# One MLP stage for two blocks: 1024 tokens with one Strassen level, u through DRAM

## The reference

```python
h = rms_norm(x, norm_mix[i])
m = rms_norm(mem, norm_mem[i])
y_mix, xq = gla_branch(h, gla_w_in[j], gla_w_gate2[j], gla_b_gate[j], gla_out_gain[j])
y_mem = memory_cross_attention(xq, m, w_kv[i])
x = x + jnp.concatenate([y_mix, y_mem.astype(y_mix.dtype)], axis=-1) @ w_out[i]
x = x + sq_relu_mlp(rms_norm(x, norm_mlp[i]), w_up[i], w_down[i])
return rms_norm(x, final_norm)

def sq_relu_mlp(h, w_up, w_down):
    u = jax.nn.relu(h @ w_up)
    return (u * u) @ w_down
```

## Time and profile before

| | |
|---|---|
| median of 3 runs | 2464.06 us (2461.39 to 2465.43) |
| span of the profiled execution, first to last instruction | 2459.9 us |
| the profiled execution's own time | its span and what lies around it; the median of the runs is 4.2 us above the span |
| TensorE busy | 2441.6 us, 99% |
| DVE busy | 1830.7 us, 74% |
| ACT busy | 1291.8 us, 53% |
| POOL busy | 312.5 us, 13% |
| DMA | 505 MB, 205 GB/s on average |

### The profile page before, as it was taken

The page is one execution under the profiler, slowest core; times in us unless marked ns, Lnnn a source line. Parts: engine busy times, 40 slices in busy tenths (PEclk is TensorE's granted clock), DMA queues, the critical chain, the costliest instruction groups (busy, mean ns, idle before and its releaser), DMA issues.

```text
span 2459.9 us, 34497 instructions
## 1 busy us (share of the span) xinstructions
PE 2441.6 (99%) x12912; PEld 2105.9 (86%) x12912; DVE 1830.7 (74%) x2671; ACT 1291.8 (53%) x2035; POOL 312.5 (13%) x327
## 2 busy tenths in 40 slices
PE   9999999999999999999999999999999999999998
PEld 8888888888788888889988888898898888889987
DVE  6677468778856788777775768877785677887777
ACT  5545354544543456566644345665665435556655
POOL 0033200000303320000020431000020142000000
PEclk9999999999999999999999999999999999999999
DMA  8964548677695444466564626355665553545554
GB/s 317 350 213 172 188 172 313 251 274 258 244 373 211 171 163 133 163 214 209 188 219 175 242 101 202 111 184 203 213 212 203 189 199 122 184 149 177 188 182 179
DMA packets 237843, 505.00 MB, mean 205 GB/s; under 512 B 12432, under 2 KB 125456, under 8 KB 219504
## 3 DMA queue, kind: packets, MB, share of 16 engines
q1 hardware_dynamic: 237248, 502.73, 58.4%
q10 hardware_dynamic: 432, 0.07, 0.0%
HBM read 423.07 MB, written 79.69 MB: 204 GB/s over the span
## 4 chain that ended last, share of the span: by engine, by line
PE 95%; DVE 2%; DMA 2%; issue 1%; ACT 0%; POOL 0%; SPq 0%; DVEq 0%; POOLq 0%; ACTq 0%
PE banks L3026 28%; PE banks L3028 28%; PE banks L3027 28%; PE banks L3216 3%; PE banks L3188 1%; PE banks L3262 1%; PE banks L3256 1%; PE banks L3165 1%; PE banks L3240 1%; DMA sr<-in_w_out 1%; PE banks L3178 0%; PE banks L3482 0%; PE banks L3274 0%; DMA xres<-in_x 0%; PE banks L3099 0%
## 5 line engine op out<-in xcount | busy, mean ns | idle before, releaser
L3026 PE MATMUL banks<-h_hi,w_hi 128*128 128x512 f32 (+1 forms) x1728 | 605.6, 350 | 2.4 <-DMA w_lo<-w_in_lo 0.8
L3028 PE MATMUL banks<-h_hi,w_lo 128*128 128x512 f32 (+1 forms) x1728 | 598.1, 346 | 0.0
L3027 PE MATMUL banks<-h_lo,w_hi 128*128 128x512 f32 (+1 forms) x1728 | 597.9, 346 | 0.0
L2833 DVE TENSOR_TENSOR w_lo<-raw,w_hi 128x1024 fp32r<-128x1024 f32 (+1 forms) x312 | 364.8, 1186 | 56.7 <-ACT w_hi L1861 56.4
L1861 ACT ACTIVATE w_hi<-raw 128x1024 fp32r<-128x1024 f32 (+1 forms) x312 | 300.9, 1003 | 166.7 <-PE banks L3026 59.4
L3026 PEld LDWEIGHTS banks<-h_hi,w_hi 128*128 128x128 f32 x1728 | 327.3, 189 | 44.1 <-issue 3.1
L3028 PEld LDWEIGHTS banks<-h_hi,w_lo 128*128 128x128 f32 x1728 | 327.2, 189 | 40.6
L3027 PEld LDWEIGHTS banks<-h_lo,w_hi 128*128 128x128 f32 x1728 | 327.5, 190 | 39.3
L3026 PE MATMUL banks<-w_hi,u_hi 128*128 128x512 f32 x896 | 350.8, 392 | 1.3 <-ACT w_hi L1401 1.0
L3028 PE MATMUL banks<-w_hi,u_lo 128*128 128x512 f32 x896 | 348.8, 389 | 0.0
L3027 PE MATMUL banks<-w_lo,u_hi 128*128 128x512 f32 x896 | 348.7, 389 | 0.0
(11 more groups left out here) (311 smaller groups left out, 4392.9 us busy)
## 6 DMA issues: line engine op xcount, KB each, us to landing
raw<-w_mix SPq DMA_DIRECT2D x52, 1024.0 KB, 4.8
raw<-in_w_down SPq DMA_DIRECT2D x48, 1024.0 KB, 5.7
raw<-w_up_mix SPq DMA_DIRECT2D x72, 512.0 KB, 4.8
w_hi<-w_in_hi SPq DMA_DIRECT2D x29, 1024.0 KB, 4.9
w_lo<-w_in_lo SPq DMA_DIRECT2D x29, 1024.0 KB, 7.9
raw<-in_w_up SPq DMA_DIRECT2D x28, 1024.0 KB, 5.6
raw<-in_gla_w_in SPq DMA_DIRECT2D x21, 1024.0 KB, 7.5
raw<-in_w_up SPq DMA_DIRECT2D x36, 512.0 KB, 4.1
```

Of the source, the lines that this page charges most:

```text
L2833: nc.vector.tensor_tensor(w_lo[:, i % 2, at], raw[:, i % 2, at], w_hi[:, i % 2, at].bitcast(F32), ALU.subtract).then_inc(lo_split.sem, 1)
L3026: after_chunk(pe.matmul(to, left[0], right[0], start=start, stop=False, skip_group_check=goes_on))
L3027: pe.matmul(to, left[0], right[1], start=False, stop=False, skip_group_check=goes_on)
L3028: return pe.matmul(to, left[1], right[0], start=False, stop=stop, skip_group_check=goes_on)
```

## The change

- The mixers and output projections of two blocks run first, then one MLP for both, `mlp(m)` for m = 0, 1, with 1024 tokens. The two blocks are the two halves of the token side, so each of the seven products of an up chunk is 128 hidden columns by 512 tokens (`up_product`). There are 112 up steps (`UP_STEPS`); chunks 0 to 2 are interleaved, chunks 3 to 15 each go M1, M2, M5, M6, M7, M3, M4. `up_bank` gives the bank: M1, M6, M7 and M4 of a chunk share one, M5 and M3 another, M2 has one of its own.
- ACT and DVE split the weights of one product at a time into a ring of eight slots (`up_high`, `up_low`), five to six steps ahead. DVE makes T1 to T4 from the raw weights every time (`up_sum`); `w_up_mix` is gone. DVE also makes S1 to S4 of h at the start of the stage (`s_sums`, `s_low`).
- u and its sums, seven operands, are stored to DRAM (`store_u`, `store_u_sums`). The down projection then runs over 28 steps (`DOWN_STEPS`, seven products by four quarters of the hidden columns); each step loads 1 MB of weights and 1 MB of u and splits both.
- The sums of `w_down` are made in MLP 0's up stage in 32 halves (`half_mix_load`, `half_mix_sums`, `half_mix_store`); before, they were made in block 0.
- All four blocks have the output projection by seven products. The even block's x rows and h columns wait in DRAM for the MLP (`x_kept`, `h_kept`). After blocks 0 and 2 no MLP follows; POOL scales the next block's columns there (`scale_columns`).

The core of the diff:

```diff
-for _g in range(GROUPS):
-    _first = 0 if _g == 0 else DEPTH * _g + 1
-    MLP += [("up", c) for c in range(_first, min(DEPTH * (_g + 1) + 1, UPS))]
-    MLP += [("down", _g, j) for j in range(len(PRODUCTS))]
-LAST_UP = MLP.index(("up", UPS - 1))
...
-LATE_MLP = []
-for _g in range(GROUPS):
-    for _c in range(DEPTH * _g, DEPTH * (_g + 1)):
-        LATE_MLP += [("up", _c)] if _c < PLAIN_UPS else [("up a", _c), ("up b", _c)]
-    LATE_MLP += [("down", _g, j) for j in range(len(PRODUCTS))]
-LATE_LAST_UP = LATE_MLP.index(("up b", UPS - 1))
...
+MLPS = BLOCKS // 2
+FIRST_UPS = 3
+UP_ORDER = ("M1", "M2", "M5", "M6", "M7", "M3", "M4")
+UP_STEPS = [(c, name) for c in range(FIRST_UPS) for name in ("M1", "M2")]
+UP_STEPS += [(c, name) for name in ("M5", "M6") for c in (2, 1, 0)]
+UP_STEPS += [(c, name) for c in (2, 1, 0) for name in ("M7", "M3", "M4")]
+UP_STEPS += [(c, name) for c in range(FIRST_UPS, UPS) for name in UP_ORDER]
+UP_AT = {step: at for at, step in enumerate(UP_STEPS)}
+UP_DONE = [c for c, name in UP_STEPS if name == "M4"]
+PART = CHUNK // KG
+RING = 2 * CHUNK // PART
+UP_LEAD = 5
+UP_SUMS = [(c, e) for c, name in UP_STEPS if name in ("M1", "M5") for e in ((T1, T3) if name == "M1" else (T2, T4))]
+UP_ENDS = {15: 2, 20: 1, 25: 0, 30: 3, 36: 4, **{UP_AT[c, "M4"] + 1: c for c in range(5, UPS)}}
+S_SUMS_AT = {0: (S1,), 1: (S3, S2), 3: (S4,)}
...
+DOWN_STEPS = [(name, quarter) for name, _, _, _ in PRODUCTS for quarter in range(QUARTERS)]
+DOWN_MIX = 2 * UPS
+DOWN_MIX_AT = {18 + 5 * j // 2: j for j in range(DOWN_MIX)}
...
+def up_bank(c, name):
+    if name == "M2":
+        return 6 + c % 2
+    turn = c if c < FIRST_UPS else (5 - c) % 3
+    return turn + (3 if name in ("M5", "M3") else 0)
...
+            def half_mix_store(j):
+                slot, c, half = j % 2, j // 2, slice(j % 2 * 256, (j % 2 + 1) * 256)
+                sp.wait_ge(half_mix_made, j + 1)
+                sp.dma_start(w_mix[:, c // DEPTH, :, c % DEPTH, half], half_mix[:, slot]).then_inc(half_mix_stored[slot], 16)
...
+            def store_u(m, c):
+                sp.wait_ge(*square_ready.at(m, UP_DONE.index(c)))
+                sp.dma_start(u_kept[:, 0:3, c, :], u[:, 0:3, :]).then_inc(u_stored.sem, 16)
+            def store_u_sums(m, c):
+                sp.wait_ge(*u_sums_ready.at(m, UP_DONE.index(c)))
+                sp.dma_start(u_kept[:, 3:OPERANDS, c, :], u[:, 3:OPERANDS, :]).then_inc(u_sums_stored.sem, 16)
...
+                sp.dma_start(u_raw[slot][:], u_kept[:, operand, DEPTH * quarter:DEPTH * (quarter + 1), :])\
+                    .then_inc(u_loaded[slot].sem, 16)
...
+                    if at - 1 in UP_ENDS:
+                        store_u(m, UP_ENDS[at - 1])
+                    if at - 3 in UP_ENDS:
+                        store_u_sums(m, UP_ENDS[at - 3])
+                    if m == 0 and at + 3 in DOWN_MIX_AT:
+                        half_mix_load(DOWN_MIX_AT[at + 3])
+                    if m == 0 and at - 1 in DOWN_MIX_AT:
+                        half_mix_store(DOWN_MIX_AT[at - 1])
...
+                    act.wait_ge(*up_sum_ready.at(m, UP_SUMS.index((c, operand))))
+                nc.scalar.activation(ring_hi[:, s % RING], up_source(c, operand), ACT.Copy).then_inc(up_hi.sem, 1)
...
+                def make_u(c):
+                    before = UP_DONE.index(c) - 1
+                    if before >= 0:
+                        act.wait_ge(*u_stored.at(m, before))
+                        act.wait_ge(*u_sums_ready.at(m, before))
+                    act.wait_ge(*mlp_full(m, ("up", c, "M4")))
+                    nc.scalar.activation(u[:, A21, :], bank(("up", c, "M4")), ACT.Relu)\
+                        .then_inc(bank_read[bank_of(("up", c, "M4"))], 1)
+                    for name in ("M2", "M7", "M3"):
+                        act.wait_ge(*mlp_read(m, ("up", c, name)))
+                    for e in range(3):
+                        last = nc.scalar.activation(u[:, e, :], up_home(c, e), ACT.Relu)
+                    last.then_inc(relu_ready.sem, 1)
+                    act.wait_ge(*mlp_read(m, ("up", c, "M4")))
+                    nc.scalar.activation(u[:, A21, :], u[:, A21, :], ACT.Square)
+                    act.wait_ge(*relu_ready.at(m, before + 1))
+                    nc.scalar.activation(u[:, 0:3, :], u[:, 0:3, :], ACT.Square).then_inc(square_ready.sem, 1)
...
+                for at, (c, name) in enumerate(UP_STEPS):
+                    if UP_LEAD < at + UP_LEAD + 1 < len(UP_STEPS):
+                        up_high(m, at + UP_LEAD + 1)
+                    if at in S_HIGHS_AT:
+                        s_high(S_HIGHS_AT[at])
+                    if name in ("M1", "M5", "M6"):
+                        keep_part(c, name)
+                    if at in UP_ENDS:
+                        make_u(UP_ENDS[at])
+                    if at == len(UP_STEPS) - 3:
+                        split_down(0)
...
+                                        ring_hi[:, s % RING].bitcast(F32), ALU.subtract).then_inc(up_lo.sem, 1)
...
+                for at, (c, name) in enumerate(UP_STEPS):
+                    for e in S_SUMS_AT.get(at, ()):
+                        s_sums(e)
+                    if at + UP_LEAD < len(UP_STEPS):
+                        up_low(m, at + UP_LEAD)
+                    if at in S_LOWS_AT:
+                        s_low(S_LOWS_AT[at])
+                    if name in ("M2", "M7", "M3"):
+                        add_part(c, name)
+                    if at - 2 in UP_ENDS:
+                        u_sums(UP_ENDS[at - 2])
+                    if m == 0 and at in DOWN_MIX_AT:
+                        half_mix_sums(DOWN_MIX_AT[at])
+                split_down(0)
+                u_sums(UPS - 1)
...
+                        pe.wait_ge(*even_low.at(m, KG - 1 if operand == A11 else KD - 1))
+                    pe.wait_ge(*mlp_empty(m, ("up", c, name)))
+                    high, low = up_operand[operand]
+                    to = bank(("up", c, name))
...
+                for s in range(len(UP_STEPS)):
+                    up_product(s)
+                    if s == 1:
+                        for g in range(KD // 2):
```

2683 lines of the change are left out of this document (1225 added, 1458 removed).

## The result

The changed kernel takes **2505.18 us** (median of 4 runs, 2500.87 to 2506.22), the kernel before, on the same chip, 2462.72 (4 runs, 2459.51 to 2465.43). The ratio is 1.0167 with a 95% interval of 1.0153 to 1.0182: 42 us slower, where 2445 was forecast and 2468 was the top of the range. The profiled executions differ by as much: spans of 2504.4 and 2459.9 us, +44.5.

What follows compares the result with a forecast made beforehand. TensorE, busy 2441.6 of 2459.9 us, was taken as the bound. Savings of 60.8, 8.2 and 1.7 against additions of 24.4, 6.2, 12.4, 6 and 2.8 gave -18.9, with 4.2 around the span 2445 us; range 2412 to 2468.

Steps and rivals of the forecast that it cites:

- What the change takes off: TensorE: up-projection matmuls 60.8 us, block 0's output projection 8.2, two old MLP-stage waits 1.7 saved.
- M6 to M7: Up stages: M7 waits for ACT's copy of M6's bank, 26 times 0.94 us, 24.4 us added (22 to 41).
- u of chunk 3: Chunk 4 of each MLP: making u in ACT's queue delays M7 by 3.1 us, 6.2 added (0 to 8).
- start of the up stage: M5 of chunk 2 waits 6.2 us for DVE's S1 low half in each MLP, 12.4 us added (9 to 18).
- Stage starts: Six places where a DVE, ACT, TensorE chain is rebuilt, 1 us each: 6 us added (3 to 13).
- half sums and DMA: MLP 0's up stage: DMA traffic of u, w_up and w_down's half sums costs 2.8 us (0 to 5.6).
- the clock in MLP 1: TensorE's granted clock: the sum held no loss for it; a fall was only Rival (c).
- rival (b): MLP 0 up: half sums become the bound, 2489 us with a chain of 16.5 us; chance 0.10.
- 3.6 us of slack by the medians: MLP 0's half sums: load 4.4, sum 1.7, store 2.6, with issues about 10 us, in a buffer's turn of 13.6.
- Rival (c): TensorE's clock falls after the two long waits, 4.7 us each, giving 2454 us; chance 0.07.
- Rival (d): Down stages: late u makes the first four steps wait some 5 us each, 2465 to 2485 us; chance 0.07.

Runs made afterwards that it cites:

- the final version: The kernel of experiment 10, timed again: 2432.49 us (4 runs), ratio 0.9875 to the kernel before.
- experiment 1: Changed kernel without the half sums of w_down, their loads and stores; down stages read plain quarters: span 2461.1 us, MLP 0 up 324.1.
- 4: Changed kernel with M7 and M4 in the bank of M5 and M3, computation changed: MLP 1 up 306.2 us instead of 324.2, MLP 0 up 358.2.
- 5: Changed kernel with M2 placed between M6 and M7, banks and computation kept: span 2479.6 us, MLP 1 up 306.0, MLP 0 up 356.3.
- experiment 6: Changed kernel with u of chunk 3 made two steps later and block 0's mixer squares one step earlier: span 2490.2 us, MLP 1 up 319.3.
- experiment 7: Changed kernel with POOL scaling only 64 of 512 columns: output projections of blocks 0 and 2 take 46.4 and 46.1 us instead of 52.3 and 52.7.
- experiment 2: Changed kernel with DVE's half-sum additions on data already in SBUF, no loads or stores: span 2463.8 us, MLP 0 up 324.3.
- experiment 10: Kernel of experiment 9 with the half sums' loads issued by POOL instead of SyncE: span 2430.1 us, MLP 0 up 316.6, MLP 1 up 306.0.
- experiment 9: Changed kernel with the order of 5, the earlier squares, and half sums from step 14 every 2.8 steps: span 2452.5 us, MLP 0 up 336.0.
- experiment 13: Kernel of experiment 10 with DVE instead of POOL scaling the next block's columns in blocks 0 and 2: span 2427.2 us, 2429.0 us in one run.

## Why the prediction was wrong

What the change takes off came as priced. Before's 3408 matmuls of 256 columns, priced at 409.0 us, take 410.3 from start to start, and after's of 512 columns are 227 ns apart wherever nothing waits. So the rows were the right price. The gap of N/2.4 + 2.5 ns that the prediction sets against them is given by the Trainium skill, "TensorE: Matmul & The Clock Gate", section "Back-to-back issue gap", for a matmul by itself, and not for a stream with weight loads as here. With the waits between M6 and M7 gone, MLP 1 up takes 306.0 us, 7.0 above its 299.0, and the final version stands 31 us below the kernel before. What it adds was 52 us in the sum and some 115 in the trace.

The table has some 101 of them; the rest is scattered.

| Term of the sum | forecast | measured | shown by |
|---|---|---|---|
| M6 to M7 | 24.4 | 26, 13 of 1.0 in each MLP | 1, 4, 5 |
| u of chunk 3 | 6.2 | 4.4, two of them 2.2 longer | 6 |
| start of the up stage | 12.4 | 7.9, two of 3.95, in another place | trace only |
| stage starts | 6 | some 20, with the clock | 6, 7 |
| half sums and DMA | 2.8 | 38.9, with the clock | 1, 2, 10 |
| the clock in MLP 1 | 0 (a rival) | 3.9 | trace only |

**The step that failed** is the rival (b)'s, "against it: 3.6 us of slack by the medians", on which the 2.8 rested: a chain of load, sum and store of about 10 us within a turn of 13.6, each buffer by itself. Two things in it were off. The store was priced by a row of 2.6 us, and landed in 5.9; the row of 5.8 for 1 MB beside it was nearer. And the queue was left out: I had "SyncE's three issues and turns" as durations, not as an order. In that order the load into one buffer waits for the landing of that buffer's last store, and meanwhile holds back the store of the other buffer: it is issued 3.9 us after its sums are through, in the mean of the middle 24 halves. A turn of a buffer is then 2 x 8.67 = 17.3 us where 13.6 was planned and 15.0 was the deciding point. The rival's own result, 2489 for a chain of 16.5, was the right mechanism with a price a little too low, and its chance of 0.10 far too low. That DVE had room was right (experiment 2). That the rate of DMA is what costs, as the 2.8 assumed, was not: its share in MLP 0 up is 0.66 with 221 GB/s, and with the same bytes the half sums cost 50.3 us over MLP 1 in 5, 29.5 in 9 and 10.6 in 10: some 21 us from the pace, 19 from the queue.

**The clock.** Rival (c) happened too, smaller apiece and in more places than priced: 1.3 to 2.9 us where 4.7 was taken, but after twelve waits rather than two. Added up it is 25 us more than before, over half of it in MLP 0, where experiment 1 left under 4 of the 13.1. So a long wait can cost more than itself, but its length alone doesn't decide: a wait of 2.10 us in experiment 7 (at 734 us) was followed by seven matmuls at 1.2 GHz, one of 3.83 us in experiment 13 (at 1512 us) by none. Which waits the clock follows stays open.

**The start of the up stage** was priced for DVE's chain to S1's low half, and TensorE was to wait for it at M5. The chain came as priced, 14.1 us where 14.6 was taken; the place of the wait was wrong. An addition in the same queue, out of a bank that M2 needs again, was late first, and while M2 waited 3.95 us and then ran partly at the lower clock, S1's low half was finished. With both, M5 starts 5.6 us late, where 6.2 was forecast; the waits alone, 7.9 for two, lie 1 us below the bounds of 9 to 18.

**Stage starts** were six at 1 us. Three long ones are no starts: in block 0's mixers ACT squares the next rows ahead of a copy that TensorE needs (7.7 us, experiment 6), and in the output projections of blocks 0 and 2 POOL's scaling slows DVE's instructions (5.9 and 6.6 us, experiment 7). Both were moved there by the change, in ACT's and in POOL's queue, and I costed neither. The slowing was to be read in the trace of before, where POOL scales in other stages: ten `w_lo` of 128x1024 of the MLPs (L2833) that lie wholly beside POOL's work have a median of 2.07 us there, those beside none of it 1.22. Rival (d) did not happen: both down stages together have 0.8 us of waits.

**Open:** MLP 0 up is still 10.6 us above MLP 1's in 10, where a buffer's own load, sum and store take longer than the pace; a third buffer was not tried. Nor was any edit for the wait at the start of the up stage, 3.8 us in each MLP; a free bank for M2 would by the times above gain little, as M5 could not start before S1's low half is there. Why a store lands in 5.9 us in this mix and in 3.2 with its load behind it isn't settled.

## What to carry to other kernels

A double buffer is only double if its loads and stores don't share an in-order queue with waits: write down the queue's order, with each wait in it, and take as the turn what one store's landing and the issues behind it add up to, with the landing of the stretch it will run in. Between two products that use one bank put a product that uses another; here that alone was worth 18 us in MLP 1. And count a long wait of TensorE with what the clock can lose after it, here another 1.3 to 2.9 us behind most waits of 3.2 us and more.

## What the runs showed that was not expected

Which queue issues was worth more than how fast a transfer is: 64 loads issued by POOL land in 4.2 us (experiment 10), by SyncE in 3.8 (experiment 9), and yet the stage is 19 us shorter. An instruction of DVE with two SBUF inputs goes from 1.22 to 2.31 us beside POOL, while one that reads a bank keeps its 0.68. And ACT, idle for over half of the span, was the worse place for these issues: MLP 0 up took 5 us more than with POOL, though DVE waited 20 us less for the loads.
